# First attention of a two-block transformer: projections packed to 128 rows, values moved to the end

## The reference

```
kv_a = hk @ w_kv_a                                # 256 latent columns and 32 rope columns
c_kv, k_rope = split(kv_a, [256]);  c_kv = rms_norm(c_kv)
kv = (c_kv @ w_kv_b).reshape(S, 16, 64 + 64)      # per head: nope key, value
k_nope = rms_norm(k_nope);  k_rope = apply_rope(rms_norm(k_rope))   # one rope key for all heads
q  = (rms_norm(h @ w_dq) @ w_uq).reshape(S, 16, 64 + 32)            # per head: nope, rope
q_nope = rms_norm(q_nope);  q_rope = apply_rope(rms_norm(q_rope))
s  = (q_nope . k_nope + q_rope . k_rope) / sqrt(96), masked by chunks of 64
o  = softmax(s) @ v;  mix = o @ w_o
```

## Time and profile before

| | |
|---|---|
| median of 3 runs | 1396.03 us (1388.57 to 1398.98) |
| the profiled execution | 1400.58 us, span 1398.9 us |
| TensorE busy | 1331.5 us, 95% of the span |
| VectorE, ScalarE, GpSimd busy | 849.2, 619.3, 33.0 us |
| mean granted TensorE clock | 0.966 of full speed |
| projections of the attention layer | about 407 to 468 us of the span |
| attention loop | about 468 to 543 us |

### The profile page before, as it was taken

One profiled execution on the slowest core, in us unless ns is written; L12 is line 12 of the kernel. 1 busy time (PEld: TensorE's weight loads), 2 busy tenths in 40 slices (PEclk: granted clock), 3 DMA queues, 4 the chain that ended last, 5 costly groups with the idle time before them and its releaser, 6 DMA issues.

```text
span 1398.9 us, 26647 instructions
## 1 busy us (share of the span) xinstructions
PE 1331.5 (95%) x11572; PEld 1226.1 (88%) x11572; DVE 849.2 (61%) x1161; ACT 619.3 (44%) x792; POOL 33.0 (2%) x40
## 2 busy tenths in 40 slices
PE   5878899999899899999999999999999999999997
PEld 4667899999854458999999999999988889999997
DVE  7896677766733666566645565446456655766543
ACT  4925443433434444544444444335333454644342
POOL 2000000000000110000000000000000000000000
PEclk8889999999999899999999999999998999999998
DMA  9864578778642471555556455454463344355452
GB/s 247 279 207 136 173 220 273 263 246 280 229 165 91 150 242 61 153 185 184 159 181 220 151 180 170 139 181 142 122 196 106 121 137 165 122 187 192 147 185 71
DMA packets 222437, 246.90 MB, mean 177 GB/s; under 512 B 5544, under 2 KB 212856, under 8 KB 222344
## 3 DMA queue, kind: packets, MB, share of 16 engines
q1 hardware_dynamic: 216168, 222.85, 49.9%
q0 software_dynamic: 5920, 22.55, 4.8%
q10 hardware_dynamic: 256, 0.14, 0.0%
HBM read 244.47 MB, written 1.05 MB: 176 GB/s over the span
## 4 chain that ended last, share of the span: by engine, by line
PE 85%; DVE 6%; ACT 4%; DMA 3%; issue 2%; POOL 0%; ACTq 0%; DVEq 0%; SPq 0%
PE PS L1617 84%; DMA RING<-in_ffn_w_down 1%; DMA RING<-in_ada_w 1%; DVE WL L965 1%; ACT PARTS L547 1%; DVE ARENA L985 1%; DVE ARENA L1398 1%; DMA H<-in_s_log_dt 0%; PE PS L2167 0%; DMA RING<-in_w_in 0%; DVE ARENA L1412 0%; ACT ARENA L657 0%; ACT ARENA L632 0%; PE PS L2074 0%; ACT ARENA L797 0%
## 5 line engine op out<-in xcount | busy, mean ns | idle before, releaser
L1617 PE MATMUL PS<-PARTS 128*128 128x256 f32 (+3 forms) x3652 | 852.1, 285 | 0.0
L1617 PEld LDWEIGHTS PS<-PARTS 128*128 128x128 f32 (+1 forms) x3652 | 629.0, 190 | 2.0 <-issue 1.2
L965 DVE TENSOR_TENSOR WL<-RING,PARTS 128x2048 fp32r<-128x2048 f32 (+2 forms) x189 | 387.6, 2053 | 283.7 <-ACT PARTS L547 283.3
L1617 PE MATMUL PS<-HH,WL 128*128 128x256 f32 (+3 forms) x1832 | 524.7, 286 | 7.5 <-DVE PARTS L945 3.0
L1617 PE MATMUL PS<-HH,PARTS 128*128 128x256 f32 (+3 forms) x1832 | 521.9, 285 | 0.0
L547 ACT CAST PARTS<-RING 128x2048 fp32r<-128x2048 f32 (+2 forms) x189 | 323.9, 1716 | 311.0 <-DMA RING<-in_w_ffn_out 67.8
L1617 PEld LDWEIGHTS PS<-HH,WL 128*128 128x128 f32 (+1 forms) x1832 | 348.7, 190 | 13.7 <-issue 7.2
L1617 PEld LDWEIGHTS PS<-HH,PARTS 128*128 128x128 f32 (+1 forms) x1832 | 348.1, 190 | 0.4
L1617 PE MATMUL PS<-PARTS,WL 128*128 128x256 f32 (+1 forms) x832 | 237.4, 285 | 1.8 <-DVE WL L965 1.4
L1617 PEld LDWEIGHTS PS<-PARTS,WL 128*128 128x128 f32 x832 | 158.8, 191 | 3.3 <-issue 2.7
L1617 PE MATMUL PS<-ARENA 128*32 128x63 f32 (+5 forms) x720 | 59.3, 262 | 2.2 <-issue 1.8
(11 more groups left out here) (293 smaller groups left out, 1034.9 us busy)
## 6 DMA issues: line engine op xcount, KB each, us to landing
RING<-in_w_ffn_in SPq DMA_DIRECT2D x44, 1024.0 KB, 5.1
RING<-in_ada_w SPq DMA_DIRECT2D x36, 1024.0 KB, 7.3
RING<-in_ffn_w_gate SPq DMA_DIRECT2D x22, 1024.0 KB, 5.3
RING<-in_ffn_w_up SPq DMA_DIRECT2D x22, 1024.0 KB, 5.4
RING<-in_w_in SPq DMA_DIRECT2D x20, 1024.0 KB, 5.3
ARENA<-in_ada_w POOLq DMA_DIRECT2D x12, 1024.0 KB, 7.5
RING<-in_ffn_w_down SPq DMA_DIRECT2D x16, 768.0 KB, 4.6
RING<-in_w_ffn_out SPq DMA_DIRECT2D x16, 768.0 KB, 4.5
```

What stands on the lines that cost most here:

```text
L965: V.tensor_tensor(WL[:, u % SLOTS, 0:w], RING[:, u % SLOTS, 0:w], WH[:, u % SLOTS, 0:w].bitcast(fp32), SUB)\
L1617: return nc.tensor.matmul(o, lhsT, rhs, start=start, stop=stop)
```

## The change

- The ring brings `uq` before `kvb`.
- New function `packed`: VectorE copies columns of the weights in the ring into tiles of their own, so that those of one kind lie side by side: WQR (rope columns of all 16 heads), WQN (nope columns of the queries), WKN (nope columns of the keys). Six copies, two per tile.
- `project(s)` runs 10 steps with 128 output rows: steps 0 and 1 make the rope rows of eight heads each (four heads a half), steps 2 to 5 the nope queries of four heads each (two heads a half), steps 6 to 9 the nope keys. Mean squares use a block matrix of 1/32 or 1/64 over all 128 rows. One Exp serves two steps.
- Raw results go to tiles RAW[s]. `normed(s)` scales the rope steps in place, and for the nope steps writes two operations of 64 rows, one for each head of a half, to rows 0 to 63 of QH or KH.
- Rope: `rotate` runs twice in all (128 x 128, 512 columns), in steps 5 and 6, `turned_q` multiplies by sine and cosine on VectorE, `roped` adds in eight operations of 32 rows into rows 64 to 95 of QH. GpSimd's cosine product is gone.
- The shared rope key lies on rows 0 to 31; the spread over all heads is written in step 3.
- The value matmuls come after the ten steps, in four halves; ScalarE copies them last.
- Scalings of steps 7, 8 and 9 and half of the second group of adds are done on VectorE inside the attention loop (h = 0 to 4); no rotation is left in the loop.

The diff, cut to its core:

```
         stream("ada_gap", ADA1, (0, KT), (ADA_MLA[0] - 12) * 512, (ADA_MLA[2] - 12) * 512, 256)
+        stream("uq", w_view("mla_w_uq", 0), (0, 2), 0, 1536, 768)
         stream("kvb", w_view("w_kv_b"), (0, 2), 0, 2048, 1024)
-        stream("uq", w_view("mla_w_uq", 0), (0, 2), 0, 1536, 768)
...
-            for s1 in range(HEADS1 // 2):
-                pool.wait_ge(S["hp_rot"], s1 + 1)
-                q = QH[NOPE:QK1, 2 * s1:2 * s1 + 2, :]
-                nc.gpsimd.tensor_tensor(q, q, COSQ[NOPE:QK1, :].unsqueeze(1).broadcast_to([ROPE, 2, SEQ]), MUL)\
-                    .then_inc(S["q_cos"], 1)
...
+            def packed(label, c, width, c0, n, dst, done):
+                u = AT[label] + c
+                dve.wait_ge(w_loaded[u % SLOTS], 16 * (u // SLOTS + 1))
+                src = slot(u, 2, 8 * width).rearrange("p k (h c) -> p k h c", c=width)[:, :, :, c0:c0 + n]
+                V.tensor_copy(dst[:, :, c * 8 * n:(c + 1) * 8 * n].rearrange("p k (h c) -> p k h c", c=n), src).then_inc(S[done], 1)
...
+            def normed(s):
+                dve.wait_ge(S["hp_std"], s // 2 + 1)
+                dve.wait_ge(S["hp_raw"], s + 1)
+                if s < 2:
+                    ins = V.scalar_tensor_tensor(RAW[s], RAW[s], vec("mla_q_rope_norm_g", 0), SDH[:, s, :], MUL, MUL)
+                else:
+                    dst, h, g = (QH, 4 * (s - 2), "mla_q_nope_norm_g") if s < 6 else (KH, 4 * (s - 6), "k_nope_norm_g")
+                    for i in range(2):
+                        r = slice(NOPE * i, NOPE * i + NOPE)
+                        ins = V.scalar_tensor_tensor(dst[0:NOPE, h + i:h + i + 3:2, :], RAW[s][r].rearrange("p (a t) -> p a t", a=2),
+                                                     VEC[r, VAT[g]:VAT[g] + 1], SDH[r, s, :].rearrange("p (a t) -> p a t", a=2), MUL, MUL)
+                ins.then_inc(S["hp_scaled"], 1)
...
+            for s in range(10):
+                raw(s)
+                if s == 2:
+                    for c in range(2):
+                        packed("kvb", c, NOPE + VDIM, 0, NOPE, WKN, "kv_packed")
+                if s == 3:
+                    dve.wait_ge(S["dve_step"], steps[0])
+                    V.tensor_copy(KH[NOPE:QK1, :, :], KR[K, 1, :].unsqueeze(1).broadcast_to([ROPE, HEADS1, SEQ])).then_inc(S["kr_done"], 1)
+                if s == 4:
+                    normed(0)
+                    normed(1)
+                if s == 5:
+                    turned_q(0)
+                if s >= 6:
+                    if s == 9:
+                        turned_q(1)
+                        roped(0, 0, 1, 2, 3)
+                    normed((2, 3, 4, 6)[s - 6])
+            normed(5)
...
-                if h % 2 == 0 and h // 2 + 2 < HEADS1 // 2:
-                    rope(h // 2 + 2)
+                if h in (0, 3, 4):
+                    normed({0: 7, 3: 8, 4: 9}[h])
+                if h in (1, 2):
+                    roped(1, 2 * h - 2, 2 * h - 1)
...
+            for s in range(10):
+                project(s)
                 if s >= 1:
                     mean_square(s - 1)
+                if s in (5, 6):
+                    rotate(s - 5)
+            pe.wait_ge(S["kr_done"], 1)
+            for n in range(4):
+                if n == 1:
+                    mean_square(9)
+                if n >= 2:
+                    pe.wait_ge(S["rope_used"], n - 1)
+                loaded(AT["kvb"] + n // 2)
+                heads = slot(AT["kvb"] + n // 2, 2, 1024).rearrange("p k (h c) -> p k h c", c=NOPE + VDIM)
+                for k in range(2):
+                    ins = mm(PS[:, V_BANK[n], :], CKV[:, k, n % 2 * P:(n % 2 + 1) * P], heads[:, k, :, NOPE:], k == 0, k == 1)
+                ins.then_inc(S["v_proj"] if n % 2 == 0 else S["unit_done"], 1)
```

More of the change, by code:

```diff
@@ L87 @@
     _n += _rows
-VAT["q96"], VAT["k96"] = _n, _n + 1
-assert VAT["norm1_g"] + 16 == P and _n + 2 <= 2 * P
+HEAD_GAINS = (("mla_q_nope_norm_g", 2), ("mla_q_rope_norm_g", 4), ("k_nope_norm_g", 2), ("k_rope_norm_g", 1))
+for _i, (_name, _) in enumerate(HEAD_GAINS):
+    VAT[_name] = _n + _i
+assert VAT["norm1_g"] + 16 == P and _n + 4 <= 2 * P
 def build(nc, A, out):
@@ L146, in build @@
         S5_AT = at
-        SDH, _ = arena(0, HEADS1, 2 * SEQ)
+        SDH, at_raw = arena(0, 10, 2 * SEQ)
+        RAW = [H[:, :, :].rearrange("p a b -> p (a b)")[:, s * 2 * SEQ:(s + 1) * 2 * SEQ] for s in range(4)] \
+            + [arena(at_raw + s * 2 * SEQ, 2 * SEQ)[0] for s in range(6)]
+        assert at_raw + 6 * 2 * SEQ <= S5_AT
         HL, at = arena(at, KT, TALL, area=PARTS)
@@ L376, in x_of @@
             return X[:, :, TALL - N_TOK[n]:TALL]
+        HP_LAST = {1: 1, 5: 2}
+        HP_COUNT = {s: s + 1 - sum(t < s for t in HP_LAST) for s in range(10)}
+        HP_GAIN = ["mla_q_rope_norm_g"] * 2 + ["mla_q_nope_norm_g"] * 4 + ["k_nope_norm_g"] * 4
+        HP_ORDER = [0, 1, 2, 3, 4, 6, 5, 7, 8, 9]
+        V_BANK = (6, 7, 4, 5)
         T_CH = CN[:, C_T:C_T + NCH].unsqueeze(1).broadcast_to([P, PAIRS, NCH])
@@ L759, in _ @@
             for b in range(3):
-                rows = P if b < 2 else QK1
+                rows = P if b < 2 else ROPE
                 nc.scalar.activation(SQ[0:rows, b, 0:SEQ], PS[0:rows, b, 0:SEQ], ACT.Square).then_inc(S["kv_sq"], 1)
@@ L778, in _ @@
                         act.wait_ge(S["hp_stat"], s - 1)
[L779 to L786, removed]
+                    nc.scalar.activation(SQH[:, s % 2, :], RAW[s], ACT.Square).then_inc(S["hp_sq"], 1)
                 if s >= 1:
                     s1 = s - 1
-                    rows = NOPE if s1 < 8 else QK1
                     act.wait_ge(S["hp_stat"], s1 + 1)
@@ L1355, in _ @@
+            steps[0] += 1
             dve.wait_ge(S["ada_cols"], ADA_LAST + 2)
             modulation(64, 72, PS[:, 6, 384:392])
-            V.tensor_copy(KH[R, :, :], KR[R, 1, :].unsqueeze(1).broadcast_to([ROPE, HEADS1, SEQ])).then_inc(S["kr_done"], 1)
-            def two(ap):
-                return ap.rearrange("p a t -> p (a t)")
-            def pair_of(s):
-                dst, g = (KH, VAT["k96"]) if s < 8 else (QH, VAT["q96"])
-                rows = NOPE if s < 8 else QK1
-                h = 2 * (s % 8)
-                return rows, two(dst[0:rows, h:h + 2, :]), g
@@ L1382, in _ @@
-            for s in range(18):
-                if s < 16:
-                    rows, v, _ = pair_of(s)
-                    if s in (11, 15):
-                        dve.wait_ge(S["unit_done"], AT["uq"] + (s - 7) // 4)
-                    else:
-                        dve.wait_ge(S["hp_proj"], s + 1 if s < 11 else s)
-                    V.tensor_copy(v, PS[0:rows, s % 2, :]).then_inc(S["hp_raw"], 1)
-                if s == 17:
-                    rope(0)
-                    rope(1)
-                if s % 4 == 1 and s >= 5:
-                    dve.wait_ge(S["hp_std"], s // 4)
-                    dve.wait_ge(S["hp_raw"], s - 1)
-                    for s1 in range(s - 5, s - 1):
-                        rows, v, g = pair_of(s1)
-                        V.scalar_tensor_tensor(v, v, VEC[0:rows, g:g + 1], SDH[0:rows, s1, :], MUL, MUL).then_inc(S["hp_scaled"], 1)
+            for c in range(2):
+                packed("uq", c, QK1, 0, NOPE, WQN, "uq_packed")
```

178 lines of the change are left out of this document (88 added, 90 removed).

## The result

The changed kernel took 1377.82 us, the median of 4 runs (1374.93 to 1380.19), beside 1396.20 for the kernel before: a ratio of 0.9869, 95% interval 0.9841 to 0.9897. Timed again twice on other chips it gave 0.9849 (0.9818 to 0.9881) and 0.9864 (0.9835 to 0.9892). It is 18 to 20 us, 1.3 to 1.5%, faster. The prediction was 1376, with a range of 1366 to 1388.

What follows compares the result with a forecast made beforehand. Bound: a chain of waits through TensorE's projections, then the attention loop's ring across engines. Gain -27.1 plus 7.5 given back is -19.6: profiled 1400.6 becomes 1381.0, less 4.6 to the median gives 1376 us, range 1366 to 1388.

Steps and rivals of the forecast that it cites:

- Item 1: Start of the projections: first mean square at 412.4 us on the old axis, nothing gained or lost.
- Item 2: TensorE from first mean square to last value matmul: 31.8 us in sum, ending at 444.2.
- Item 3: VectorE and ScalarE during the ten steps: their work, 2.2 and 2.3 us, fits under TensorE's 2.59 us a step.
- Item 4: VectorE's work behind projection 9: first score's inputs ready at 441.4, 2.8 us before TensorE is free.
- Item 5: First score of the attention: its copy begins at about 445.1 instead of 472.20, a gain of 27.1 us.
- The attention: Attention loop without rotations: TensorE's stands grow from 0.61 to 1.55 us; 2.5 new clock falls at 3.0 us, +7.5 us.
- The step from one profile to the median: Whole run: profiled 1400.6 us becomes 1381.0, and the same 4.6 us above the median gives 1376.
- The clock holds: Rival, attention loop: stands grow but no new clock fall comes; 1369 us, chance 0.20.
- Falls in all four pairs: Rival, attention loop: the clock falls in the pairs of heads 4, 6, 8 and 10; 1381 to 1389 us, chance 0.20.
- VectorE feeds too slowly: Rival, start and steps 2 and 3: packs at upper bound, first mean square at 413.6; +2.5, 1379 us, chance 0.07.
- Low clock throughout: Rival, attention: the low clock stays through all of it, +32 against -27.1; 1401 us, chance 0.03.
- no effect: Rival, packed projections: a matmul with twice the columns takes twice as long; 1396 us, chance 0.02.

Runs made afterwards that it cites:

- kernel with all stands filled: Changed kernel plus idle 512-column matmuls: two ahead of projection 0, two ahead of head 2's score, one ahead of heads 4, 6, 8, 10, 12; 1365.54 and 1366.30 us.
- double pack: Changed kernel with VectorE making both packs of the nope key columns twice, 1.3 us more in step 2; 1374.00 us in one run.
- values in the middle: Changed kernel with two value halves behind step 6 and two behind step 8, instead of all behind step 9; 1378.95 and 1383.74 us.
- filled kernel: Changed kernel with one idle matmul of 512 columns ahead of the scores of heads 2, 4, 6, 8, 10 and 12; 1369.89 and 1367.62 us.
- half fills: Changed kernel with idle matmuls of 256 columns in the attention loop ahead of the scores of heads 2, 4, 6, 8, 10 and 12; 1378.74 us in one run.
- kernel before, filled: Kernel before the change with one idle matmul of 512 columns ahead of the scores of heads 2 and 12; 1393.78 us, ratio 0.9987.

## Why the prediction was right, point by point

**Item 1, the start, failed by 2 to 4 us.** It had the first mean square 14.6 us behind the statistics; it came at 16.8, and at 18.6 and 18.7 in the other two executions of the changed kernel. Two terms were too small. The second query unit was to land at 407.2, 9.4 us behind the statistics; it landed at 412.9, 11.2 behind. The chain of waits, with the pack behind it (start, us, what):

```profile
406.19 6.73 DMA RING<-in_mla_w_uq
...
412.95 0.44 DVE ARENA L1366
```

Two stretches of that transfer by busy time (the last two columns are DMA share and GB/s):

```profile
408.00:411.00 3.00, 3.00 (x34) 2.19 (x26) 0.80 (x2) 0.58 (x1) 0.00 (x0) 1.00 0.99 304
411.00:414.00 3.00, 0.76 (x2) 0.51 (x2) 1.05 (x3) 0.00 (x0) 0.00 (x0) 0.86 1.02 391
```

By the rates, the engines moved 2.02 MB from 406.00 to 412.92, and the two query units are 1.57. The other 0.45 MB would be, but for a possible rest of the ada unit ahead, the next units of the ring, issued at 407.96; at the 400 GB/s of the last stretch they make 1.1 of the 1.8 us. That is an estimate; no run took those units away. The prediction took the rate of the earlier trace rows and gave all of it to the two units that it was asking about. In the other two executions the second unit landed still later, 12.0 and 12.3 us behind the statistics. The second term is the clock: behind the stand of 2.24 us projections 0 and 1 took 5.25 us (PEclk 0.58 from 414 to 417), and not the 3.67 of the earlier trace rows. The 3.90 us at full clock in the kernel with all stands filled shows that it was the clock; in the second and third execution of the changed kernel they took 6.32 and 6.00. The kernel before had a fall here too, one step later: its second group of projections took 3.53 us instead of 1.94, at 0.56. The prediction named that fall, but set its own start and its own steps at full clock. In the table the fall has moved one line up, from behind the first mean square to ahead of it. The packs cost what was reckoned: 0.43 us for 512 elements and 0.65 each for 1024, estimated 0.4 and 0.7. So the operation of the lower bound, L1357, was the one to take the price from the earlier trace rows. The page "VectorE: DVE Perf Modes" of the Trainium skill, section "Mode 2×_2P — use both read ports for one tensor", has such copies at two elements a cycle, and this trace agrees, also for packs that gather columns with gaps between them (0.63 ns an element against 1.34 from PSUM).

**Item 2, TensorE's list, right.** 31.8 us from the first mean square to the last value matmul; 30.98 measured to the first score, which follows it without a stand. Ten steps stand for sixteen at the same price each.

**Item 3, VectorE beside it, right**, and the double pack shows the room.

**Item 4, the tail of VectorE, right in kind, its room smaller.** VectorE's last work in the changed kernel:

```profile
441.11 0.69 DVE L1388 COPY ARENA<-PS 128x512 f32<-128x512 f32 x1 [0.35 <-PE PS L1662]
...
443.15 2.78 DVE L1419 TENSOR_TENSOR ARENA<-ARENA,H 32x512 f32<-32x512 f32 x4
445.96 3.05 DVE L1400 SCALAR_TENSOR_TENSOR ARENA<-ARENA,VEC 64x512 f32<-64x512 f32 x4
450.35 0.56 DVE L1455 SCALAR_TENSOR_TENSOR ARENA<-PS,CN 128x384 f32<-128x384 f32 x1 [1.34 <-PE PS L1662]
```

The first two scalings end at about 447.5, 2.0 us ahead of the score at 449.49, where 2.8 were reckoned. With the values in the middle the tail took the predicted 6.4 us and TensorE stood. Split scalings take 3.05 us for four; four of one start row took 2.74 in the kernel before. The prediction had 0.07 us of loss for each, measured is 0.10. The same page, section "Two Vector instructions with no wait between them", has an instruction whose inputs or output start in another quadrant wait for the earlier ones. The 0.10 us fits that, but no run here isolates it; the loss lay beside TensorE.

**Item 5, the gain of 27.1 us, right.** Counted from the first mean square it is 28.0, of which 1.6 are the fall that moved ahead of it. Counted from the statistics it is 25.8, because of item 1.

**The attention, right in mechanism and in count of new falls; the size was wrong.** The stands grew from 0.61 to 1.39 us (1.55 predicted), and of the four pairs that could newly fall, three fell in the first execution of the changed kernel, three in the second, two in the third: 2.7 in the mean, 2.5 predicted. The size is the term that failed. A fall in the changed kernel costs 9.9 - 8.28 = 1.6 us; 3.0 was taken from a fall of the kernel before, which cost 3.2. The falls of heads 2 and 12 were also kept at their old size, but these, too, went from 3.2 to 1.6. So three new falls gave +4.9, the two old ones -3.2, together +1.7 in place of +7.5. In the second execution head 2 had no fall at all behind its 2.17 us (its pair took 7.49 us). In that one and the third, the way from the column matmuls of head 2 to `WL` took 65.1 and 65.0 us, as long as the 65.15 of the kernel before: nothing was given back. Why the old falls were twice as dear can be read in the granted clock. Behind head 2 of the kernel before, on both sides of the stretch with 0.50 in the earlier trace rows:

```profile
477.00:480.00 3.00, 2.26 (x15) 1.96 (x19) 2.79 (x9) 1.62 (x7) 0.00 (x0) 0.68 0.77 242
...
483.00:486.00 3.00, 3.00 (x19) 1.88 (x11) 0.77 (x3) 0.00 (x0) 0.00 (x0) 0.68 0.97 319
```

Behind head 6 of the changed kernel, following the stretch 474 to 477 with 0.60:

```profile
477.00:480.00 3.00, 3.00 (x35) 1.71 (x27) 0.11 (x1) 0.00 (x0) 0.00 (x0) 0.84 0.21 38
```

A mean of 0.68 over 3 us is 1.9 us at the lower level, so the clock was low for 1.9 + 3.0 + 1.9 = 6.8 us there, and for 2.4 + 1.0 = 3.4 us here. Half of that is lost, 3.4 and 1.7 us by this working against 3.2 and 1.6 measured. Both lengths occur in both kernels: the fall of the kernel before at its first mean square (413) lasted 3.4 us, those around projections 0 and 1 in the second and third execution of the changed kernel 6.8. So the price of a fall goes with how long the clock stays low, and the prediction took its one price from a long fall. What decides the length was not found.

**The step from one profile to the median** was wrong in the other direction. The prediction subtracted from the profiled 1400.6 and then took off the 4.6 us by which that execution lay above its median. The sum of -19.6 was 3.0 short of the 22.6 between the spans, but the profiled execution of the changed kernel lay only 0.1 above its own median. That these two cancel to under 2 us is luck, and so is a part of the 3.0 itself: the stretch ahead of the statistics and the start took 6.2 us more than forecast, the attention, the steps and the rest 9.2 less. With the medians alone the gain is 18.4 us, 18.5 and 20.2 in the three comparisons.

**The rivals.** "The clock holds", 1369: false for this kernel, and the filled kernel shows that its price was right (1367.6 and 1369.9). "Falls in all four pairs": three of them at most. "VectorE feeds too slowly": the first mean square did come later than its 413.6 on the old axis, but for the transfer and the clock, not for the packs; no ada unit was late. "Low clock throughout" and "no effect": false.

## What to carry to other kernels

In these runs a matmul's price went by its moving columns and not by its output rows (64, 96 or 128), so pack heads until the output rows are full; but first look at what the removed matmuls were doing for the clock, and where a stand of about 1 us repeats in a loop (0.95 to 1.48 here), try one idle matmul in it. Move independent TensorE work (here the values) behind the last step whose result VectorE must still finish. When a transfer is timed by its share of a rate, allow for the units queued behind it; that they took part of it here is an estimate.

## What the runs showed of the hardware that was not expected

- Stands of 0.95 to 1.48 us, one in each pair of heads of 8.3 us, were enough for a fall of the clock to 1.2 GHz in two or three of the four pairs of heads 4 to 10. Behind stands of 0.45 to 0.61 us there was none, in five profiled executions with the loop filled and in two of the kernel before, with and without its fills. Each fall in the loop of the changed kernel cost about 1.6 us. The page "TensorE: Matmul & The Clock Gate" of the Trainium skill, section "A second HAM failure mode: psum-queue depth-cycling", tells of short idle times between groups of matmuls that make the clock swing between its two levels; the trace agrees in kind.
- Not every longer stand is followed by a fall. In the loops of the seven profiled executions in which every stand was 0.95 us or longer (three of the changed kernel, one with double packs, two with the values in the middle, one with half fills) 31 of 42 stands were followed by one. The pair of head 4 kept the full clock in the first and third execution of the changed kernel and lost it in the second (9.94 us), where the pairs of heads 2 and 8 kept it, head 2 behind 2.17 us. Stands of 0.88 us (head 2 of the kernel before, filled) and 1.14 us (ahead of projection 0, all stands filled) were not followed by one either.
- A fall can also come without a stand right ahead of it: in the first run with all stands filled the clock went low 5.4 us behind the last stand, inside the idle matmuls. What decides wasn't found.
- A fall cost 3.2 us in the loop of the kernel before and 1.6 in that of the changed one, because the clock stayed low for 6.8 and for 3.4 us.
